# Two transformer blocks in split fp32: the high and low halves of stationary weights stored side by side

## The chip, the cores and the metric

The kernel runs on one core of a Trainium2 chip. The metric is the device time of one execution in microseconds. The kernel before took 1435.29 us (median of three runs, 1434.83 to 1439.27).

## The reference

Two models follow each other on 256 rows of 1024 features. All is fp32. The first block is a mixer (pooling and windowed attention) and an MLP:

```python
h2 = _rmsnorm(x, g_mlp_pre[l])
ff = jnp.einsum('bsf,fd->bsd',
                jnp.square(jax.nn.relu(jnp.einsum('bsd,df->bsf', h2, w_up[l]))), w_down[l])
x = x + _rmsnorm(ff, g_mlp_post[l])
```

The second has two layers, on 256 latent rows and 256 context rows. Layer 0 is a short convolution and a gated feed-forward on both sets of rows; layer 1 is attention with compressed keys and a feed-forward on the latent rows alone:

```python
def swiglu(h, w_gate, w_up, w_down):
    return (jax.nn.silu(h @ w_gate) * (h @ w_up)) @ w_down

def short_conv_mixer(h, w_in, conv_k, conv_b, w_out):
    b_gate, c_gate, u = jnp.split(h @ w_in, 3, axis=-1)
    z = c_gate * u
    ...
    return (b_gate * y) @ w_out
```

## The kernel before, in words

**Split products.** The operands of every weight product are split into two parts of type fp32r: `hi` is the value rounded to that type, `lo` is what the rounding left. `product` then runs three matmuls a term: hi by hi (line 454), one of the lo parts by the other's hi (line 455), and the other way round (line 456). All three accumulate in one PSUM bank.

**Weight chunks.** Weights come in chunks of up to 128 x 4096 fp32 (2 MiB), in the order of `STREAM`. SyncE loads chunk after chunk into the two slots of `raw`. ScalarE copies a chunk into `w_hi` (line 980, two halves), VectorE subtracts and writes `w_lo` (line 1432, two halves). `w_hi` and `w_lo` have two slots each. ScalarE may write a slot once TensorE is through with the chunk before last (`gemm_done`). SyncE may refill a slot of `raw` once VectorE is through with it (`lo_ready`). TensorE waits for the first half of `lo` in `chunk` and for the second in the middle of its first product. Chunks of modulation weights are read by TensorE from `raw` and are not split.

**Stationary and moving.** A matmul first loads a stationary operand (128 columns, the PEld rows of the profile), then streams a moving one. In the trace's names the moving operand stands first: `bank<-act_hi,w_hi` has the weights stationary. They are stationary where the result is wanted with features on partitions:

- `up` (8 chunks of the MLP), 96 matmuls a chunk, moving operand 256 columns
- `conv_in` (8 chunks of 72 matmuls a pass: the first chunk in two passes of 256 columns, the other seven in one of 512)
- `gate_up` (the feed-forward of layer 0: one chunk in two passes of 256 columns, ten chunks of 96 matmuls with 512 columns)
- `gate_up1` (the feed-forward of layer 1: 11 chunks, 96 matmuls each, 256 columns)

In all other products (projections, `down`, `down0`, `down1`, `conv_out`, attention) the activations are stationary and the weights stream.

**Order.** Each engine's program is written by hand, and semaphores join them. ScalarE and VectorE have, between the splits, the activation functions, the splits of activations, the norms and the sums. A split stands in VectorE's queue where the code puts it, so at the ends of stages it can stand ahead of the sums that the next norm needs.

Of the kernel before, what the change touches and what calls it, by code (L numbers as in the profile page):

```python
# [16 lines left out]
P = 128  # L17
D = 1024
KT = D // P
SEQ = 256  # L20
NT = SEQ // P
CHUNK = 4096
COLS = 512
# [68 lines left out]
STREAM = _stream()  # L92
WEIGHT_AT = [i for i, c in enumerate(STREAM) if not c[3]]
MOD_AT = [i for i, c in enumerate(STREAM) if c[3]]
WEIGHTS = len(WEIGHT_AT)
X_UPDATES = 16
UNITS_BEFORE_CONV = 2 * 3 + 2 + 2 * 4 + 8 + 2 + 8 + 4 + 4 * 8

# [57 lines left out]
def build(nc, a, out):  # L156
    f32, f32r = mybir.dt.float32, mybir.dt.float32r
    ACT, ALU, AX = mybir.ActivationFunctionType, mybir.AluOpType, mybir.AxisListType
# [4 lines left out]
    def at(name, shape, offset, dtype=f32):  # L163
        return nc.alloc_sbuf_tensor_at(name, shape, dtype, offset=base + offset)

    K = 1024
    raw = at("raw", [P, 2, CHUNK], 0)
    w_hi = at("w_hi", [P, 2, CHUNK], 32 * K, f32r)
    w_lo = at("w_lo", [P, 2, CHUNK], 64 * K, f32r)
    x = at("x", [P, NT, D], 96 * K)  # L170
    ACT0 = 104 * K
    act_hi = at("act_hi", [P, 2, KT, SEQ], ACT0, f32r)
    act_lo = at("act_lo", [P, 2, KT, SEQ], ACT0 + 16 * K, f32r)
# [44 lines left out]
    mlp = at("mlp", [P, NT, D], PH + 24 * K)  # L218
# [49 lines left out]
    def table(name, n, parts=P, j=0):  # L268
        return tab[0:parts, TAB[name] + j:TAB[name] + j + n]
# [18 lines left out]
    hi_ready = S("hi_ready")  # L288
# [52 lines left out]

    WQ, WKV = QKT * GH * QK, KVT * COLS

    def halves_of(width):


        half = width // 2
        return [(h * half, (h + 1) * half) for h in range(2)]

    with nc.Block() as block:  # L350
# [3 lines left out]
        def _(sp):  # L354
# [37 lines left out]
            for t in range(NT):  # L392
                sp.wait_ge(x_ready, X_UPDATES - NT + 1 + t)
                sp.dma_start(out[t * P:(t + 1) * P, :], x[:, t, :]).then_inc(out_done, 16)
# [21 lines left out]
        def _(te):  # L416
            n = Count()

            def chunk():
                n.step("chunk")  # L420
                split_half(1)
                return (n.n["chunk"] - 1) % 2
# [3 lines left out]
                te.wait_ge(lo_ready, 2 * n.at("chunk") - back)  # L426

            def weights(s, j0, j1):
                return w_hi[:, s, j0:j1], w_lo[:, s, j0:j1]

            rot = {"first": 0, "banks": 4}

# [5 lines left out]
            def unit():  # L438
                n.step("unit")
                if n.n["unit"] > rot["banks"]:  # L440
                    te.wait_ge(gemm_read, n.at("unit", rot["banks"]))
                return bank[(n.n["unit"] - 1 - rot["first"]) % rot["banks"]]
# [31 lines left out]
            def turn_rows(buf):  # L474
                te.wait_ge(xn_ready, n.step("xn"))
                for half in range(2):
                    turn([xn[:, buf, (4 * half + j) * P:(4 * half + j + 1) * P] for j in range(4)])
# [39 lines left out]
            for k, width in enumerate((COLS, COLS, 256)):  # L517
                s = chunk()
# [113 lines left out]
            def up(first=False):  # L632

                s = chunk()
                if first:
                    te.wait_ge(norm_ready, n.step("norm", 4))
                for pair in range(2):
                    b = unit()
                    for f in (2 * pair, 2 * pair + 1):
                        last = product(b[:, (f % 2) * SEQ:(f % 2 + 1) * SEQ],  # L640
                                       [(weights(s, j * COLS + f * P, j * COLS + (f + 1) * P), (act_hi[:, 0, j, :], act_lo[:, 0, j, :]))
                                        for j in range(KT)], second=4 if f == 0 else None)
                    last.then_inc(gemm_done, 1)
                n.step("hidden", 2)
# [31 lines left out]
            def moving(k):  # L676
                return act_hi[:, :, k, :], act_lo[:, :, k, :]

            def conv_weights(s, part):
                return [weights(s, k * 384 + part * P, k * 384 + (part + 1) * P) for k in range(KT)]  # L680

            def conv_in():
                s = chunk()
# [9 lines left out]
            s = chunk()  # L693
# [48 lines left out]
            s = chunk()  # L742
            for tt in range(2 * NT):
                conv_out(s, tt, tt == 0)
            s = chunk()
            norm_both(lambda tt: conv_out(s, tt, False), True)

            def gate_up(apart=False):

                s = chunk()  # L750
                for f in range(2):
                    for part in range(2):
                        b = unit()
                        cols_of = [weights(s, k * COLS + part * 256 + f * P, k * COLS + part * 256 + (f + 1) * P) for k in range(KT)]
                        half = 4 if f == part == 0 else None
                        if apart:
                            product(b[:, 0:SEQ], [(cols_of[k], (act_hi[:, 0, k, :], act_lo[:, 0, k, :])) for k in range(KT)], second=half)
                            if f == 0:
                                turn_rows(part)
                        else:  # L760
                            product(b[:, :].rearrange("p (s t) -> p s t", s=2), [(cols_of[k], moving(k)) for k in range(KT)],
                                    second=half).then_inc(gemm_done, 1)
                if apart:
                    mod_product(1, 2)
                    te.wait_ge(norm_ready, n.step("norm", 4))
                    for f in range(2):
                        for part in range(2):
                            cols_of = [weights(s, k * COLS + part * 256 + f * P, k * COLS + part * 256 + (f + 1) * P) for k in range(KT)]
                            product(bank[2 * f + part][:, SEQ:2 * SEQ], [(cols_of[k], (act_hi[:, 1, k, :], act_lo[:, 1, k, :])) for k in range(KT)]
                                    ).then_inc(gemm_done, 1)  # L770
                            gate_rows(4, f, part)
# [33 lines left out]
            s = chunk()  # L805
# [7 lines left out]
            for c in range(3):  # L813
                s = chunk()
                for tt in range(2 * NT if c == 2 else NT):
# [3 lines left out]
                    first = 0 if tt < NT else MLA_W - KVL - ROPE  # L819
# [19 lines left out]
            held = {}  # L839
# [78 lines left out]
            def gate_up1():  # L918

                s = chunk()  # L920
                for f in range(2):
                    b = unit()
                    for part in range(2):
                        first = part * 256 + f * P
                        last = product(b[:, part * SEQ:(part + 1) * SEQ],
                                       [(weights(s, j * COLS + first, j * COLS + first + P), (act_hi[:, 0, j, :], act_lo[:, 0, j, :]))
                                        for j in range(KT)], second=4 if f == part == 0 else None)
                    last.then_inc(gemm_done, 1)
                n.step("hidden", 2)
# [25 lines left out]
            down1(1, 2, 0)  # L955
            assert n.n["chunk"] == WEIGHTS and n.n["mod"] == len(MOD_AT) and n.n["batch"] == 8


        @block.scalar
        def _(act):  # L960
            n = Count()

            def split(width=CHUNK, rest=None):
                n.step("split")
                c = n.n["split"]
                if c > WEIGHTS:
                    return
                assert STREAM[WEIGHT_AT[c - 1]][2] == width, (c, width)
                s, at = (c - 1) % 2, WEIGHT_AT[c - 1]
                turns = 16 * (at // 2 + 1)  # L970
                if n.turn is not None:
                    turns = n.turn * (8 * n.per["split"]) + turns
                act.wait_ge(loaded[at % 2], turns)
                if rest is not None:
                    act.wait_ge(rest_loaded[rest], 16)
                if n.n["unit"]:
                    act.wait_ge(gemm_done, n.at("unit"))
                for first, end in halves_of(width):
                    part = slice(first, end)
                    act.activation(w_hi[:, s, part], raw[:, at % 2, part], ACT.Copy).then_inc(hi_ready, 1)  # L980

            def roots(sources, width):

# [432 lines left out]
        def _(ve):  # L1416
# [7 lines left out]
            def split(width=CHUNK):  # L1424
                n.step("split")
                if n.n["split"] > WEIGHTS:
                    return
                s, at = (n.n["split"] - 1) % 2, WEIGHT_AT[n.n["split"] - 1]
                for half, (first, end) in enumerate(halves_of(width)):
                    part = slice(first, end)  # L1430
                    ve.wait_ge(hi_ready, 2 * n.at("split") - 1 + half)
                    ve.tensor_tensor(w_lo[:, s, part], raw[:, at % 2, part], w_hi[:, s, part].bitcast(f32),  # L1432
                                     ALU.subtract).then_inc(lo_ready, 1)

            rot = {"first": 0, "banks": 4}
# [124 lines left out]
            for t in range(NT):  # L1560
# [3 lines left out]
                s = table("sin1", 8, j=8 * t).rearrange("p (o d) -> p o d", o=1).to_broadcast([P, 10, 8])  # L1564
# [634 lines left out]
```

## Time and profile before

| | |
|---|---|
| median of three runs | 1435.29 us |
| profiled execution, its own time | 1439.03 us |
| its span, first to last instruction | 1437.2 us |
| mean granted TensorE clock | 0.975 |
| TensorE busy, share of the span | 93% |
| TensorE's weight load busy | 78% |
| VectorE, ScalarE busy | 56%, 38% |
| mean of the DMA | 152 GB/s |

The profiled execution is 1.8 us longer than its span, and 3.7 us over the median of the runs. The duration of one matmul in the trace includes its latency, so neighbours overlap; the pace of a stream is read from the starts of the first and the last matmul. The granted clock is 1.00 at 2.4 GHz and 0.50 at 1.2 GHz.

### The profile page before, as it was taken

To read this page: it belongs to the slowest core of one execution; us is meant where nothing else is said; L and a number is where in the kernel's file an instruction comes from. 1 tells how busy PE (TensorE), PEld (TensorE's weight loads), DVE (VectorE), ACT (ScalarE), POOL (GpSimd) and SP (SyncE) were. 2 spreads that over 40 slices of the span, in tenths; PEclk is the share of its full clock that TensorE was granted. 3 is DMA by queue.
4 is the path that set the end of the run, shared out by engine and by line. 5 is a ranking of instruction groups with operands and counts; after the bars stand their busy time and mean duration, and the time that the engine had idled before them with its cause. 6 is when DMAs were issued, how large, how long until landed. Compare 5 with 4: busy or idle time off the path is not lost.

```text
span 1437.2 us, 17619 instructions
## 1 busy us (share of the span) xinstructions
PE 1342.5 (93%) x7376; PEld 1116.1 (78%) x7376; DVE 803.8 (56%) x1087; ACT 544.6 (38%) x679; POOL 3.5 (0%) x10
## 2 busy tenths in 40 slices
PE   5999779999999999999999999998789988799998
PEld 4877678899777788877777777887667766699997
DVE  5666565458664455662525252537556664656666
ACT  5353343454431123422121212125455552544432
POOL 0000000000000000000000000000000000000000
PEclk9999979999999999999999999999889998899999
DMA  8536436545644532363535353412121311345441
GB/s 307 192 117 251 174 110 249 213 176 180 230 154 197 205 117 88 135 245 127 226 124 227 124 227 125 150 43 92 33 87 48 117 59 59 117 159 194 175 175 59
DMA packets 23782, 218.80 MB, mean 152 GB/s; under 512 B 3104, under 2 KB 8224, under 8 KB 10656
## 3 DMA queue, kind: packets, MB, share of 16 engines
q1 hardware_dynamic: 21328, 209.67, 40.2%
q10 hardware_dynamic: 1520, 4.98, 0.9%
q0 software_dynamic: 864, 3.15, 0.7%
q8 instruction: 53, 0.87, 0.2%
q14 instruction: 17, 0.14, 0.0%
HBM read 216.74 MB, written 1.05 MB: 152 GB/s over the span
## 4 chain that ended last, share of the span: by engine, by line
PE 77%; DVE 12%; ACT 7%; issue 3%; DMA 1%; ACTq 0%; DVEq 0%
PE bank L454 23%; PE bank L455 22%; PE bank L456 22%; DVE w_lo L1432 4%; PE turned L471 3%; PE mod_ps L492 3%; ACT w_hi L980 2%; DVE scaled L1473 2%; PE bank L861 2%; PE small L867 2%; DVE gated L1778 1%; DMA raw<-in_w_branch 1%; ACT xn L987 1%; PE small L511 1%; DMA raw<-in_w_out 1%
## 5 line engine op out<-in xcount | busy, mean ns | idle before, releaser
L454 PE MATMUL bank<-act_hi,w_hi 128*128 128x256 f32 (+1 forms) x1208 | 399.7, 331 | 8.8 <-DVE act_lo L1457 6.3
L455 PE MATMUL bank<-act_lo,w_hi 128*128 128x256 f32 (+1 forms) x1208 | 395.8, 328 | 0.0
L456 PE MATMUL bank<-act_hi,w_lo 128*128 128x256 f32 (+1 forms) x1208 | 395.5, 327 | 0.0
L1432 DVE TENSOR_TENSOR w_lo<-raw,w_hi 128x2048 fp32r<-128x2048 f32 (+4 forms) x168 | 338.2, 2055 | 89.8 <-ACT w_hi L980 89.7
L980 ACT ACTIVATE w_hi<-raw 128x2048 fp32r<-128x2048 f32 (+4 forms) x168 | 280.1, 1715 | 210.0 <-PE bank L456 169.7
L454 PEld LDWEIGHTS bank<-act_hi,w_hi 128*128 128x128 f32 x1208 | 231.8, 192 | 42.8 <-issue 17.0
L455 PEld LDWEIGHTS bank<-act_lo,w_hi 128*128 128x128 f32 x1208 | 232.0, 192 | 19.5 <-issue 0.7
L456 PEld LDWEIGHTS bank<-act_hi,w_lo 128*128 128x128 f32 x1208 | 231.8, 192 | 19.3
L454 PE MATMUL bank<-w_hi,h_hi 128*128 128x512 f32 x392 | 155.4, 396 | 4.0 <-DVE h_lo L1830 2.3
L455 PE MATMUL bank<-w_lo,h_hi 128*128 128x512 f32 x392 | 153.4, 391 | 0.0
L456 PE MATMUL bank<-w_hi,h_lo 128*128 128x512 f32 x392 | 153.3, 391 | 0.0
L454 PE MATMUL bank<-w_hi,act_hi 128*128 128x512 f32 (+3 forms) x240 | 92.2, 384 | 9.6 <-DVE w_lo L1432 5.6
L454 PEld LDWEIGHTS bank<-w_hi,h_hi 128*128 128x128 f32 x392 | 74.0, 189 | 26.5 <-issue 7.7
L1827 DVE TENSOR_TENSOR h<-silu,bank 128x512 f32<-128x512 f32 x22 | 15.1, 688 | 141.5 <-PE bank L456 141.5
L455 PE MATMUL bank<-w_lo,act_hi 128*128 128x512 f32 (+3 forms) x240 | 89.5, 373 | 0.0
L456 PE MATMUL bank<-w_hi,act_lo 128*128 128x512 f32 (+3 forms) x240 | 89.4, 372 | 0.0
L1778 DVE TENSOR_TENSOR gated<-bank,gate 128x512 f32<-128x512 f32 x84 | 57.8, 688 | 53.6 <-PE bank L456 53.4
L456 PEld LDWEIGHTS bank<-w_hi,h_lo 128*128 128x128 f32 x392 | 74.0, 189 | 15.8
L455 PEld LDWEIGHTS bank<-w_lo,h_hi 128*128 128x128 f32 x392 | 74.1, 189 | 14.9 <-issue 0.2
L454 PEld LDWEIGHTS bank<-w_hi,act_hi 128*128 128x128 f32 x240 | 46.8, 195 | 19.3 <-DVE w_lo L1432 6.3
L1254 ACT ACTIVATE h_hi<-h 128x512 fp32r<-128x512 f32 x22 | 13.9, 631 | 122.2 <-DVE h L1827 122.2
L471 PE MATMUL turned<-tab,xn 128*128 128x128 f32 x156 | 24.9, 311 | 30.5 <-ACT xn L996 27.2
(227 smaller groups left out, 1421.5 us busy)
## 6 DMA issues: line engine op xcount, KB each, us to landing
raw<-in_ffn SPq DMA_DIRECT2D x35, 2048.0 KB, 8.1
raw<-in_mlp SPq DMA_DIRECT2D x24, 2048.0 KB, 8.0
raw<-in_mod_gate SPq DMA_DIRECT2D x7, 2048.0 KB, 8.1
raw<-in_conv_in SPq DMA_DIRECT2D x8, 1536.0 KB, 7.1
raw<-in_w_gates SPq DMA_DIRECT2D x4, 2048.0 KB, 8.5
raw<-in_w_branch SPq DMA_DIRECT2D x4, 2048.0 KB, 7.9
raw<-in_mla_q SPq DMA_DIRECT2D x4, 1152.0 KB, 5.3
raw<-in_w_in SPq DMA_DIRECT2D x2, 2048.0 KB, 14.0
```

The lines of the kernel that those rows point to most:

```text
L454: te.matmul(dst, sh, mh, start=(j == 0), stop=False)
L455: te.matmul(dst, sh, ml, start=False, stop=False)
L456: last = te.matmul(dst, sl, mh, start=False, stop=(j == len(terms) - 1))
L471: last = te.transpose(dst[0:m, j * P:(j + 1) * P], src, ident)
L492: last = te.matmul(mod_ps[q:q + 32, :], cond[:, k, 6 - 2 * j:38 - 2 * j], raw[:, slot, k * COLS:(k + 1) * COLS], start=(j == 0 and k < 4), ...
L861: te.matmul(bank[u % 2][:, :], qgT[:, h, t * P:(t + 1) * P], kgT[:, h, :], start=True, stop=True).then_inc(scores_done, 1)
L867: last = te.matmul(small[:, u * VD:(u + 1) * VD], prT[:, u % 2, j, :], vg[:, j, h, :], start=(j == 0), stop=(j == 3))
L980: act.activation(w_hi[:, s, part], raw[:, at % 2, part], ACT.Copy).then_inc(hi_ready, 1)
L1432: ve.tensor_tensor(w_lo[:, s, part], raw[:, at % 2, part], w_hi[:, s, part].bitcast(f32), ALU.subtract).then_inc(lo_ready, 1)
L1473: last = ve.tensor_scalar(dst[:, j, :], src[:, j, :], gain[:, j, :], shift[:, j, :], ALU.mult, ALU.add)
L1778: ve.tensor_tensor(gated[:, k, :], b[:, :], gate[:, g, cb * COLS:(cb + 1) * COLS], ALU.mult).then_inc(gemm_read, 1)
L1827: ve.tensor_tensor(h2[:, f, :], silu[:, f, :], b[:, :], ALU.mult).then_inc(gemm_read, 2)
```

## The change

The two tensors `w_hi` and `w_lo` become one region of 64 KiB a partition, with 32 KiB a slot. It has two views. `w_apart` holds the hi part of a chunk and then its lo part, each contiguous. `w_pair` holds hi and lo of an element next to each other, so that one part is read and written with a step of two elements (8 bytes). A function `held` tells by section and number which view a chunk has: the MLP's up chunks, `conv_in`, and the gate and up chunks of both feed-forwards are in pairs, all others apart. In the list above these are 38 chunks; 76 of the 168 split instructions on ScalarE and as many on VectorE write (and VectorE reads) with the step, and 3624 weight loads of TensorE read with it. The number, the order, the shapes and the waits of the instructions are the same on all engines.

```diff
+FFN1_DOWN = (4, 7, 10, 13, 15)
+def held(section, k):
+
+    if section == "mlp":
+        return k % 6 < 4
+    if section == "ffn0":
+        return k % 4 in (0, 2) and k != 18 or k == 17
+    if section == "ffn1":
+        return k not in FFN1_DOWN
+    return section in ("conv_in", "ffn0_first")
...
-    w_hi = at("w_hi", [P, 2, CHUNK], 32 * K, f32r)
-    w_lo = at("w_lo", [P, 2, CHUNK], 64 * K, f32r)
+    w_apart = at("w_apart", [P, 2, 2, CHUNK], 32 * K, f32r)
+    w_pair = at("w_pair", [P, 2, CHUNK, 2], 32 * K, f32r)
...
+    def high_half(at, s, part):
+        section, k = STREAM[at][0:2]
+        return w_pair[:, s, part, 0] if held(section, k) else w_apart[:, s, 0, part]
+
+    def low_half(at, s, part):
+        section, k = STREAM[at][0:2]
+        return w_pair[:, s, part, 1] if held(section, k) else w_apart[:, s, 1, part]
...
             def weights(s, j0, j1):
-                return w_hi[:, s, j0:j1], w_lo[:, s, j0:j1]
+                return w_apart[:, s, 0, j0:j1], w_apart[:, s, 1, j0:j1]
+
+            def held_weights(s, j0, j1):
+
+                return w_pair[:, s, j0:j1, 0], w_pair[:, s, j0:j1, 1]
...
-                                       [(weights(s, j * COLS + f * P, j * COLS + (f + 1) * P), (act_hi[:, 0, j, :], act_lo[:, 0, j, :]))
+                                       [(held_weights(s, j * COLS + f * P, j * COLS + (f + 1) * P), (act_hi[:, 0, j, :], act_lo[:, 0, j, :]))
...
-                    act.activation(w_hi[:, s, part], raw[:, at % 2, part], ACT.Copy).then_inc(hi_ready, 1)
+                    act.activation(high_half(at, s, part), raw[:, at % 2, part], ACT.Copy).then_inc(hi_ready, 1)
...
-                    ve.tensor_tensor(w_lo[:, s, part], raw[:, at % 2, part], w_hi[:, s, part].bitcast(f32),
+                    ve.tensor_tensor(low_half(at, s, part), raw[:, at % 2, part], high_half(at, s, part).bitcast(f32),
```

The same replacement of `weights` by `held_weights` stands in `conv_weights`, `gate_up` (two places) and `gate_up1`.

## Rows read from the trace of the kernel before

**Rows 1.** The page: busy time, and the chain that ended last.

```profile
PE 1342.5 (93%) x7376; PEld 1116.1 (78%) x7376; DVE 803.8 (56%) x1087; ACT 544.6 (38%) x679; POOL 3.5 (0%) x10
...
PE 77%; DVE 12%; ACT 7%; issue 3%; DMA 1%; ACTq 0%; DVEq 0%
```

**Rows 2.** Waits of TensorE: us in total, times, longest.

```profile
PE bank L454 <- DVE w_lo L1432: 7.5, 3, 3.7
```

**Rows 3.** Groups by shape: count, busy us, mean ns; of each triple the first.

```profile
L1432 DVE TENSOR_TENSOR w_lo<-raw,w_hi 128x2048 fp32r<-128x2048 f32 x124 | 278.5, 2288 | 75.8 <-ACT w_hi L980 75.8
...
L980 ACT ACTIVATE w_hi<-raw 128x2048 fp32r<-128x2048 f32 x124 | 230.0, 1903 | 200.1 <-PE bank L456 159.9 <-DMA raw<-in_mlp 14.1 <-DMA raw<-in_ffn 10.9
L454 PE MATMUL bank<-act_hi,w_hi 128*128 128x256 f32 x720 | 208.2, 289 | 8.8 <-DVE act_lo L1457 6.3 <-issue 2.5
...
L454 PE MATMUL bank<-act_hi,w_hi 128*128 128x512 f32 x488 | 191.5, 392 | 0.0
```

**Rows 4.** TensorE in order of time: start, us; held weights, 256 columns, full clock.

```profile
1257.78 0.28 PE L454 MATMUL bank<-act_hi,w_hi 128*128 128x256 f32 x1
...
1271.70 0.28 PE L456 MATMUL bank<-act_hi,w_lo 128*128 128x256 f32 x1
```

**Rows 5.** The same, held weights, 512 columns, full clock.

```profile
657.02 0.39 PE L455 MATMUL bank<-act_lo,w_hi 128*128 128x512 f32 x1
...
678.35 0.39 PE L456 MATMUL bank<-act_hi,w_lo 128*128 128x512 f32 x1
```

**Rows 6.** The same, held weights, 256 columns, half clock.

```profile
191.92 0.41 PE L456 MATMUL bank<-act_hi,w_lo 128*128 128x256 f32 x1
...
196.82 0.36 PE L455 MATMUL bank<-act_lo,w_hi 128*128 128x256 f32 x1
```

**Rows 7.** Stretches: length, busy PE, PEld, DVE, ACT, POOL, granted clock, DMA.

```profile
640.00:900.00 260.00, 260.00 (x1226) 200.17 (x1225) 102.58 (x106) 60.55 (x56) 0.00 (x0) 1.00 0.48 173
191.70:196.80 5.10, 5.10 (x25) 5.10 (x25) 5.07 (x3) 2.42 (x2) 0.00 (x0) 0.50 0.00 0
1258.00:1284.00 26.00, 26.00 (x219) 26.00 (x218) 13.25 (x15) 12.90 (x16) 0.00 (x0) 1.00 0.44 163
...
1243.90:1248.40 4.50, 4.50 (x21) 4.50 (x22) 3.46 (x2) 4.09 (x3) 0.00 (x0) 0.51 0.02 4
```

**Rows 8.** In order of time: eight transposes; seven weight loads with 64 moving columns each.

```profile
577.38 1.03 PE L471 MATMUL turned<-tab,xn 128*128 128x128 f32 x8
...
1112.46 0.86 PEld L867 LDWEIGHTS small<-vg,prT 128*128 128x128 f32 x7 [0.24 <-issue]
```

**Rows 9.** Groups: VectorE reductions of 128 elements, first with, second without a step.

```profile
L1513 DVE TENSOR_REDUCE fold<-turned 128x32 f32<-128x128 f32 x4 | 1.1, 284 | 0.0
...
L1889 DVE TENSOR_REDUCE stat<-pe_t 128x4 f32<-128x128 f32 x1 | 0.3, 286 | 0.0
```

**Rows 10.** ScalarE and VectorE in order of time, feed-forward of layer 1.

```profile
1258.89 3.70 ACT L980 ACTIVATE w_hi<-raw 128x2048 fp32r<-128x2048 f32 x2
...
1260.82 4.49 DVE L1432 TENSOR_TENSOR w_lo<-raw,w_hi 128x2048 fp32r<-128x2048 f32 x2 [1.38 <-ACT w_hi L980]
...
1270.41 3.71 ACT L980 ACTIVATE w_hi<-raw 128x2048 fp32r<-128x2048 f32 x2
```

**Rows 11.** The chain in order of time: start, us, what.

```profile
165.08 1.93 ACT w_hi L980
167.10 3.38 DVE w_lo L1432 x2
...
559.96 1.93 ACT w_hi L980
561.92 3.48 DVE w_lo L1432 x2
...
1222.27 1.93 ACT w_hi L980
1224.22 4.49 DVE w_lo L1432 x2
```

**Rows 12.** DMA issues: count, KB each, us to landing.

```profile
raw<-in_ffn SPq DMA_DIRECT2D x35, 2048.0 KB, 8.1
```

More of the change, by code:

```diff
@@ L679, in conv_weights @@
             def conv_weights(s, part):
-                return [weights(s, k * 384 + part * P, k * 384 + (part + 1) * P) for k in range(KT)]
+                return [held_weights(s, k * 384 + part * P, k * 384 + (part + 1) * P) for k in range(KT)]
             def conv_in():
@@ L753, in gate_up @@
                         b = unit()
-                        cols_of = [weights(s, k * COLS + part * 256 + f * P, k * COLS + part * 256 + (f + 1) * P) for k in range(KT)]
+                        cols_of = [held_weights(s, k * COLS + part * 256 + f * P, k * COLS + part * 256 + (f + 1) * P) for k in range(KT)]
                         half = 4 if f == part == 0 else None
@@ L767, in gate_up @@
                         for part in range(2):
-                            cols_of = [weights(s, k * COLS + part * 256 + f * P, k * COLS + part * 256 + (f + 1) * P) for k in range(KT)]
+                            cols_of = [held_weights(s, k * COLS + part * 256 + f * P, k * COLS + part * 256 + (f + 1) * P) for k in range(KT)]
                             product(bank[2 * f + part][:, SEQ:2 * SEQ], [(cols_of[k], (act_hi[:, 1, k, :], act_lo[:, 1, k, :])) for k in range(KT)]
@@ L925, in gate_up1 @@
                         last = product(b[:, part * SEQ:(part + 1) * SEQ],
-                                       [(weights(s, j * COLS + first, j * COLS + first + P), (act_hi[:, 0, j, :], act_lo[:, 0, j, :]))
+                                       [(held_weights(s, j * COLS + first, j * COLS + first + P), (act_hi[:, 0, j, :], act_lo[:, 0, j, :]))
                                         for j in range(KT)], second=4 if f == part == 0 else None)
```

## The prediction

> **What bounds the kernel now.** I read the page's busy times and its chain first: TensorE is busy for 93% of the span and carries 77% of the chain, VectorE 12% and ScalarE 7% [rows 1]. TensorE's waits come next: all its waits for the lo part of a weight chunk are 7.5 us, in three places [rows 2]. So in the long stages the end is set by how fast TensorE runs its matmuls, and the splits run beside it. The stretches say the same: in 640 to 900 us and in 1258 to 1284 us TensorE is busy for the whole stretch at a granted clock of 1.00, and VectorE for 39% and 51% of it [rows 7].
>
> What the change touches on TensorE is counted in the groups by shape: 720 triples with 256 moving columns and 488 triples with 512 have the weights stationary, so 2160 and 1464 matmuls, each with its own load [rows 3]. Their pace is read from starts. With 256 columns, 116 intervals lie between 1257.78 and 1271.70: 13.92 us / 116 = 120.0 ns [rows 4]. With 512, 94 intervals (the rest of a chunk of 96 matmuls) take 21.33 us: 226.9 ns [rows 5]. The columns alone need 256/2.4 = 106.7 ns and 512/2.4 = 213.3 ns. So each matmul has a surcharge of 13.3 and 13.6 ns that does not grow with its columns. At the granted clock of 0.50 (1.2 GHz) it is gone: 23 intervals in 4.90 us are 213.0 ns, and 256/1.2 is 213.3 ns [rows 6, 7]. Something that is no part of the array's own work, and that has room at half clock, costs 13.3 ns at full clock. In all it is 3624 x 13.3 ns = 48.2 us, 3.3% of the run. That is the largest thing the change can give on TensorE.
>
> **Part 1, the stationary load reads with a step of 8 bytes.** The trace has no such load, so this is bounded from both sides.
> How fast a load goes at best is seen where almost nothing streams: seven loads with 64 moving columns take 0.86 us. Less the 0.19 us of the last one, that is 0.67/6 = 112 ns for 128 columns. Eight transposes take (1.03 - 0.28)/7 = 107 ns each [rows 8]. So a load reads some 512 bytes in 107 to 112 ns, 4.6 to 4.8 bytes per ns and partition, and the moving stream reads 1024 bytes in 106.7 ns, 9.6 bytes per ns. The two run at the same time, through the same memory, and the load walks its addresses at half the pace of the stream. A surcharge that depends on neither width nor, at half clock, exists at all fits two readers that run into each other again and again while one overtakes the other. With a step of 8 bytes the load walks 1024 bytes in the same time, at the stream's own pace: once they are out of each other's way they stay so. That is an inference and not a row. It gives a gain of up to the whole surcharge. Against that stands the other reading of the same rows, a fixed gap between two moving streams, which a step in the load doesn't touch: gain zero. And the load now covers twice the memory: if the surcharge is paid per stretch of memory touched, it doubles.
> Gain if the first holds: with 512 columns I take 12 of the 13.6 ns, 1464 x 12 = 17.6 us. With 256 columns the load's own pace comes next: from 120.0 to 109 ns (the middle of 107 and 112), 2160 x 11 = 23.8 us. Some 46 matmuls run at half clock and gain nothing (25 and 21 in two stretches [rows 7]): -0.5 us. Sum 40.9 us.
>
> The Trainium skill ("SBUF — State Buffer", section "Who interferes with whom") says that TensorE has two independent read ports, one for the moving operand and one for the load, and never waits on anyone. By that rule the surcharge is no meeting of the two reads, and the whole change is worth nothing: the time would stay that of before. The trace neither shows nor excludes it, so it bears on the chance of "no change" below.
>
> **Part 2, ScalarE and VectorE write with the step, and VectorE reads with it.** 76 of the 168 splits on each. A half of 2048 elements now takes 2288 ns on VectorE and 1903 ns on ScalarE [rows 3]. The nearest row for a step is a reduction of 128 elements 32 words apart (in PSUM): 284 ns, against 286 ns without a step [rows 9]. So I take zero. The lower end is also zero: nothing is removed. As the upper end I take double time, since each half now lies over twice the memory.
> What hides it is seen in the feed-forward of layer 1: a split starts on ScalarE at 1258.89 and the next at 1270.41, 11.5 us apart, one chunk of 96 x 120 ns. The hi halves end 3.7 us after the start, the lo halves 6.4 us after it (1260.82 + 4.49 = 1265.31) [rows 10]. TensorE wants the chunk some 10.3 us after that start and its second half 1.4 us later (12 matmuls at 120 ns): 5 us of slack, 4 us if TensorE's chunk shrinks to 10.5 us. The DMA has 8.1 us to land [rows 12] within two chunks. Nothing else becomes late.
> If the cover goes, it goes first at the three stage ends where a held chunk's split stands in the chain: 1.93 + 3.38, 1.93 + 3.48 and 1.93 + 4.49 us, together 17.1 us [rows 11]. At double time these cost 17 us more. Between stages the second lo half would come 1.9 x 2 + 4.5 x 2 = 12.8 us after the start, against 11.7 wanted: 1.1 us on each of 19 chunks with 256 columns (mlp and layer 1), 21 us. So the upper end of part 2 is +38 us.
>
> The Trainium skill has two rules on it that differ. "SBUF — State Buffer", section "Specifications (TRN2)", wants at least two accesses to a 16-byte line for full bandwidth; a step of 8 bytes has exactly two, so it would be free, and the reduction's row doesn't contradict. "Vector Engine (DVE) Microarchitecture Reference", section 5.2, measured 1.7 times the duration where the destination hops with every 4-byte element; at that factor the three stage ends would cost 12 us, which is my rival on that side in kind.
>
> **Part 3, the other chunks.** Their halves are contiguous as before; only the distance from hi to lo is 16 KiB instead of 32. Zero, both ends.
>
> **The sum.** 1439.0 (profiled) - 40.9 + 0 = 1398.1 us. The median of the runs is 3.7 us below the profiled execution, so 1394.4 us. At stage ends and in the last MLP turn the chain goes through the splits and sums, and there TensorE's gain is partly waited away; I give 3 us back for it: 1398 us is the forecast.
>
> **The rivals.**
> No change. The surcharge is a gap between moving streams or a cost of changing the weights, whatever their layout. For it: it is the same for widths of 256 and 512. Against: it vanishes at half clock, where a cost of the array would double. Time 1435.3 us, give or take 3.
> Slower, by the load's reach. The surcharge is paid per stretch of memory that a load touches, and the stretch doubles from 512 to 1024 bytes: +13.3 ns on all 3624 matmuls, +48 us, 1484 us. It decides from the first held chunk on, in every one. For it: a fixed surcharge on a fixed load. Against: nothing in particular.
> Slower, by the splits. Part 2 between 1.7 times and double: +12 to +38 us, 1447 to 1473 us. Against it stands the reduction's row.
> Slower, by the load's pace. If a stepped load needs double time, 107 ns become 213, hidden under 512 columns (226.9 ns) but not under 256: there 120 becomes 227, 2160 x 107 ns = +231 us, 1666 us. The unstepped load already goes at half the stream's byte rate, so I hold it for unlikely.
>
> **How the numbers follow.** My forecast (a gain on TensorE) 0.50; no change 0.28; load's reach 0.10; splits 0.08; load's pace 0.04. A measurement of this kernel tells about 0.3% from no change (4.3 us). So faster 0.50, same 0.28, slower 0.22. The forecast's own range is 1385 (the whole 48 us and nothing given back) to 1420 (a third of it). The range that holds 8 in 10 also takes in no change and the small end of the splits: 1385 to 1446.
>
> **What would show each step right or wrong.** Starts of held matmuls at 109 ns and 215 ns in place of 120 and 227, with the moving-weight products still at 226 to 227, show part 1; unchanged paces show the fixed gap; 133 and 240 show the reach; 227 with 256 columns shows the load's pace. The groups of the splits at 2288 and 1903 ns with the step show part 2 right; 3.9 us and more shows it wrong. The forecast fails if the paces move and the span doesn't: then the splits or the DMA must stand in TensorE's waits.

## The result, and the profile after

The changed kernel is slower: 1450.32 us (median of 5 runs, 1448.77 to 1453.27) against 1439.27 us for the kernel before on the same chip (5 runs, 1434.83 to 1441.97). The ratio is 1.0084, 95% interval 1.0067 to 1.0101. The forecast was 1398 us, and 1450.3 lies above its range as well. The profiled span went from 1437.2 to 1447.0 us, +9.8 us, at nearly the same mean granted clock (0.975 before, 0.972 after).

The page of the changed kernel, busy time and chain, which answer to [rows 1]:

```profile
PE 1352.9 (94%) x7376; PEld 1125.2 (78%) x7376; DVE 803.6 (56%) x1087; ACT 558.5 (39%) x679; POOL 3.5 (0%) x10
...
PE 76%; DVE 12%; ACT 7%; issue 3%; DMA 2%; ACTq 0%; DVEq 0%
```

TensorE is busy 10.4 us longer and ScalarE 13.9 us; VectorE is unchanged. TensorE's waits for lo parts have not moved, 7.5 us as in [rows 2] (waits: us in total, times, longest):

```profile
PE bank L480 <- DVE w_apart L1458: 7.5, 3, 3.7
```

So it is the matmuls, not the splits. The groups by shape of the changed kernel, which answer to [rows 3]:

```profile
L480 PE MATMUL bank<-act_hi,w_pair 128*128 128x256 f32 x720 | 208.8, 290 | 8.4 <-DVE act_lo L1483 5.9 <-issue 2.5
...
L480 PE MATMUL bank<-act_hi,w_pair 128*128 128x512 f32 x488 | 193.8, 397 | 0.0
...
L1458 DVE TENSOR_TENSOR w_apart<-raw,w_apart 128x2048 fp32r<-128x2048 f32 x64 | 143.7, 2287 | 39.5 <-ACT w_apart L1006 39.5
L1458 DVE TENSOR_TENSOR w_pair<-raw,w_pair 128x2048 fp32r<-128x2048 f32 x60 | 134.8, 2290 | 41.6 <-ACT w_pair L1006 41.6
L1006 ACT ACTIVATE w_pair<-raw 128x2048 fp32r<-128x2048 f32 x60 | 122.9, 2104 | 165.3 <-PE bank L482 140.5 <-DMA raw<-in_mlp 14.3 <-DMA raw<-in_ffn 10.5
L1006 ACT ACTIVATE w_apart<-raw 128x2048 fp32r<-128x2048 f32 x64 | 118.6, 1902 | 30.5 <-PE bank L482 14.5 <-PE bank L559 6.5 <-DMA raw<-in_w_branch 6.0
```

The products with 256 columns are as they were (290 against 289 ns), those with 512 last 397 against 392 ns. VectorE's stepped halves take 2290 against 2287 ns: free. ScalarE's take 2104 against 1902 ns: +10.6%, 202 ns each.

A matmul's own duration overlaps its neighbours', so the pace is again read from starts. The changed kernel with 256 columns, to be held against [rows 4] (start, us, ...):

```profile
1265.09 0.28 PE L481 MATMUL bank<-act_lo,w_pair 128*128 128x256 f32 x1
...
1279.97 0.28 PE L482 MATMUL bank<-act_hi,w_pair 128*128 128x256 f32 x1
```

124 intervals in 14.88 us are 120.0 ns, exactly as before. With 512 columns, against [rows 5]:

```profile
663.17 0.39 PE L482 MATMUL bank<-act_hi,w_pair 128*128 128x512 f32 x1
...
684.17 0.40 PE L482 MATMUL bank<-act_hi,w_pair 128*128 128x512 f32 x1
```

90 intervals in 21.00 us are 233.3 ns; before they were 226.9. That is +6.4 ns, and 1464 x 6.4 ns = 9.4 us, nearly the whole +9.8 us of the span. The stage can be cut out of both traces. The first held product with 512 columns and the first matmul behind the last one, before:

```profile
410.14 0.50 PE L454 MATMUL bank<-act_hi,w_hi 128*128 128x512 f32 x1
...
961.66 0.39 PE L454 MATMUL bank<-w_hi,h_hi 128*128 128x512 f32 x1
```

and after:

```profile
411.49 0.50 PE L480 MATMUL bank<-act_hi,w_pair 128*128 128x512 f32 x1
...
972.17 0.39 PE L480 MATMUL bank<-w_apart,h_hi 128*128 128x512 f32 x1
```

Between them lie 551.5 us before and 560.7 after: +9.2 us. What comes ahead took 1.4 us longer, what comes behind 0.7 us less. The 1.4 us ahead are the clock's: behind its waits at the start of the convolution, TensorE ran 17 matmuls with 256 columns at a granted clock of 0.50 in this execution, 0.21 us apart in place of 0.12. The same products of the kernel before ran at 1.00. The stretch (length, busy PE, PEld, DVE, ACT, POOL, granted clock, DMA):

```profile
400.90:404.20 3.30, 3.30 (x17) 3.30 (x17) 3.10 (x5) 0.68 (x1) 0.00 (x0) 0.50 0.00 0
```

At the three stage ends, the chain of the changed kernel, which answers to [rows 11]:

```profile
164.76 2.07 ACT w_pair L1006
...
166.92 3.25 DVE w_pair L1458 x2
...
564.41 2.08 ACT w_pair L1006
...
1232.13 2.09 ACT w_pair L1006
...
1234.24 4.50 DVE w_pair L1458 x2
```

ScalarE's part grew by 0.14 to 0.16 us at each, under 0.5 us in all.

### The profile page after: what moved, and what is told of

The parts are those of the page before. It is cut to its first block, busy times and chain, and to the rows that moved or that the text cites. A ratio compares the mean times of both kernels' runs of the same rounds, so it can differ in the third digit from the quotient of the medians.

```text
span 1447.0 us, 17619 instructions
## 1 busy us (share of the span) xinstructions
PE 1352.9 (94%) x7376; PEld 1125.2 (78%) x7376; DVE 803.6 (56%) x1087; ACT 558.5 (39%) x679; POOL 3.5 (0%) x10
## 3 DMA queue, kind: packets, MB, share of 16 engines
HBM read 216.74 MB, written 1.05 MB: 151 GB/s over the span
## 4 chain that ended last, share of the span: by engine, by line
PE 76%; DVE 12%; ACT 7%; issue 3%; DMA 2%; ACTq 0%; DVEq 0%
PE bank L480 23%; PE bank L481 22%; PE bank L482 22%; DVE w_apart L1458 3%; PE turned L497 3%; PE mod_ps L518 3%; ACT w_apart L1006 2%; DVE scaled L1499 2%; DVE w_pair L1458 2%; PE bank L887 2%; PE small L893 2%; ACT w_pair L1006 1%; DVE gated L1804 1%; DMA raw<-in_w_branch 1%; ACT xn L1013 1%
## 5 line engine op out<-in xcount | busy, mean ns | idle before, releaser
L480 PE MATMUL bank<-act_hi,w_pair 128*128 128x256 f32 (+1 forms) x1208 | 402.6, 333 | 8.4 <-DVE act_lo L1483 5.9
L481 PE MATMUL bank<-act_lo,w_pair 128*128 128x256 f32 (+1 forms) x1208 | 398.4, 330 | 0.0
L482 PE MATMUL bank<-act_hi,w_pair 128*128 128x256 f32 (+1 forms) x1208 | 398.3, 330 | 0.0
L480 PEld LDWEIGHTS bank<-act_hi,w_pair 128*128 128x128 f32 x1208 | 237.5, 197 | 42.9 <-issue 17.0
L481 PEld LDWEIGHTS bank<-act_lo,w_pair 128*128 128x128 f32 x1208 | 237.7, 197 | 19.9 <-issue 0.7
L482 PEld LDWEIGHTS bank<-act_hi,w_pair 128*128 128x128 f32 x1208 | 237.4, 196 | 19.5
L1006 ACT ACTIVATE w_pair<-raw 128x2048 fp32r<-128x2048 f32 (+1 forms) x76 | 148.2, 2005 | 171.1 <-PE bank L482 146.3
L1458 DVE TENSOR_TENSOR w_apart<-raw,w_apart 128x2048 fp32r<-128x2048 f32 (+4 forms) x92 | 175.9, 1954 | 47.8 <-ACT w_apart L1006 47.7
L1458 DVE TENSOR_TENSOR w_pair<-raw,w_pair 128x2048 fp32r<-128x2048 f32 (+1 forms) x76 | 162.3, 2178 | 48.5 <-ACT w_pair L1006 48.5
L480 PE MATMUL bank<-w_apart,h_hi 128*128 128x512 f32 x392 | 154.8, 395 | 5.7 <-DVE h_lo L1856 2.3
L481 PE MATMUL bank<-w_apart,h_hi 128*128 128x512 f32 x392 | 152.7, 390 | 0.0
L482 PE MATMUL bank<-w_apart,h_lo 128*128 128x512 f32 x392 | 152.7, 390 | 0.0
L480 PE MATMUL bank<-w_apart,act_hi 128*128 128x512 f32 (+3 forms) x240 | 92.4, 385 | 9.6 <-DVE w_apart L1458 5.6
L481 PE MATMUL bank<-w_apart,act_hi 128*128 128x512 f32 (+3 forms) x240 | 89.6, 373 | 0.0
L1280 ACT ACTIVATE h_hi<-h 128x512 fp32r<-128x512 f32 x22 | 13.9, 633 | 125.4 <-DVE h L1853 125.4
```

The costliest lines, as they stand in the source:

```text
L480: te.matmul(dst, sh, mh, start=(j == 0), stop=False)
L481: te.matmul(dst, sh, ml, start=False, stop=False)
L482: last = te.matmul(dst, sl, mh, start=False, stop=(j == len(terms) - 1))
L1006: act.activation(high_half(at, s, part), raw[:, at % 2, part], ACT.Copy).then_inc(hi_ready, 1)
L1458: ve.tensor_tensor(low_half(at, s, part), raw[:, at % 2, part], high_half(at, s, part).bitcast(f32), ALU.subtract).then_inc(lo_ready, 1)
```

## Experiments

The prediction's theory was that a stepped load runs in step with the stream and removes the surcharge of 13.3 ns. The profile after had already refuted it, since no pace went down. The question became why 512 columns rose by 6.4 ns and 256 did not, and whether the surcharge has to do with addresses at all. The rival was that it is a fixed gap that no layout moves, with the loss coming from somewhere else (the new places of the halves, or ScalarE).

**The pace by itself.** A program of matmul bursts: the same stationary block and the same moving columns, 36 times, with the step, the width or the distance of the two start addresses changed from burst to burst.

```
for n, steps in ((256, (1, 2, 4)), (384, (1, 2)), (512, (1, 2, 4, 8))):
    for step in steps:
        configs.append([(stat(W, step), mov(M, n), n)] * R)
```

> A program of its own that leaves out the whole model: it streams bursts of 36 to 48 matmuls on operands at rest, no other engine at work, and then runs ScalarE copies and VectorE subtractions with and without a step. Theory A (the step of the stationary load alone costs, when the moving operand is 512 wide): a step of 2 gives 233 ns against 227 at 512 columns in one piece, and 120 against 120 at 256. Theory B (it is the moving operand in two pieces together with the step): 227 and 227 in one piece, 227 and 233 in two pieces. Theory C (addresses of the two operands relative to each other): the pace changes with the offset of the stationary operand at step 1 too, between 120 and 133, 227 and 240. Theory D (the surcharge needs the other engines or the DMA): 227 in all cases, whatever the step. ScalarE: 1.90 us without a step, 2.10 with a step of 2; VectorE 2.29 us in both.

Its TensorE in order of time; each burst (bank) stands between two small marks, and its pace is the start of the next mark less its own start, over 36:

```profile
42.38 4.56 PE L267 MATMUL bank<-mem 128*128 128x256 f32 x36
46.77 0.31 PE L264 MATMUL mark<-mem 128*128 128x64 f32 x2
46.91 4.57 PE L267 MATMUL bank<-mem 128*128 128x256 f32 x36
51.32 0.31 PE L264 MATMUL mark<-mem 128*128 128x64 f32 x2
51.46 8.65 PE L267 MATMUL bank<-mem 128*128 128x256 f32 x36
59.95 0.30 PE L264 MATMUL mark<-mem 128*128 128x64 f32 x2
...
73.02 8.43 PE L267 MATMUL bank<-mem 128*128 128x512 f32 x36
81.29 0.30 PE L264 MATMUL mark<-mem 128*128 128x64 f32 x2
81.43 8.65 PE L267 MATMUL bank<-mem 128*128 128x512 f32 x36
89.92 0.30 PE L264 MATMUL mark<-mem 128*128 128x64 f32 x2
90.05 8.82 PE L267 MATMUL bank<-mem 128*128 128x512 f32 x36
98.71 0.30 PE L264 MATMUL mark<-mem 128*128 128x64 f32 x2
```

With 256 columns: 121.9 ns without a step, 122.5 with a step of 2 elements, 235.8 with 4. With 512: 229.7, 235.8 and 240.6. (Such a burst reads some 2 ns too long, since its first matmul starts slowly: the kernel's 120.0 is 121.9 here. The granted clock is 1.00 throughout.) So both of the kernel's numbers are here with no split, no DMA and no other engine at work: a step of 2 costs 0.6 ns at 256 and 6.1 ns at 512. With the 512 columns in two pieces of 256, as in the kernel, it is 229.4 without and 235.6 with the step, so the two pieces are not the cause. Without a step, moving the stationary block by 4, 8, 16 or 32 elements gave 235.8, 235.8, 235.3 and 234.7 ns at 512 as well; by 64, 128, 256, 1024 or 4096 elements 229.2 to 229.4. So the pace with 512 columns depends on where the load starts, modulo 64 elements (256 bytes). That it is the distance to the stream, and not the load's own alignment, is shown by the bursts under "Which distances". With a step, no distance gave less than 232.8.

A half of 2048 elements copied by ScalarE took 1.91 us without a step, 2.04 us (+6.6%) with a step of 2, and 3.81 us with a step of 4; VectorE took 2.29 us in every form, steps of 1 and 2 in its input and its output.

**The new places, without pairs.** The layout of the changed kernel, but every chunk apart, and TensorE's loads with it. (This edit and the next two are shown against the changed kernel.)

```
-    if section == "mlp":
-        return k % 6 < 4
...
-    return section in ("conv_in", "ffn0_first")
+    return False
```

> The memory layout of the change (hi and lo of a slot 16 KiB apart) with no chunk in pairs. If the step is the cause: as before, 1439 us within 0.3%, held matmuls with 512 columns at 227 ns. If the nearness of hi and lo is the cause: as the change, 1450 us and 233 ns.

1439.29 us, ratio 0.9998 (0.9986 to 1.0011). In order of time:

```profile
657.45 0.40 PE L476 MATMUL bank<-act_hi,w_apart 128*128 128x512 f32 x1
...
678.55 0.39 PE L476 MATMUL bank<-act_hi,w_apart 128*128 128x512 f32 x1
```

93 intervals in 21.10 us are 226.9 ns. Part 3 of the prediction stands: the distance of 16 KiB costs nothing that these runs show.

**Pairs only where 256 columns stream** (the MLP and layer 1).

```
-    return section in ("conv_in", "ffn0_first")
+    return section == "mlp" and k % 6 < 4 or section == "ffn1" and k not in FFN1_DOWN
```

> Pairs only where the held matmuls have 256 columns throughout (MLP up, feed-forward of layer 1). If the cost is the 6.4 ns on each of the 1464 matmuls with 512 columns: as before, 1439 to 1441 us. If ScalarE's slower stepped write (2.10 against 1.90 us a half) at the ends of stages is the cause: 0.4 us at each of two stage ends, 1440 us, and the rest of the 11 us unexplained. If the whole change costs evenly per held matmul: 1439 + 11 x 1824/3624 = 1444.5 us.

1439.59 us, ratio 1.0006 (0.9995 to 1.0016); pace 120.0 ns. ScalarE paid its +10.6% here too, on 38 of the 76 stepped halves, and nothing came of it: the split's cover held.

**Pairs only where 512 columns stream** (the convolution's input and the feed-forward of layer 0).

```
-    if section == "mlp":
-        return k % 6 < 4
...
-    if section == "ffn1":
-        return k not in FFN1_DOWN
```

> Pairs only in conv_in and in the gate and up chunks of layer 0, where 1464 of 1800 held matmuls have 512 columns. If those 1464 x 6.4 ns = 9.4 us are the cause: 1448 to 1450 us, nearly the whole loss. If the cost is even per held matmul: 1444.5 us.

1447.81 us, ratio 1.0054 (1.0041 to 1.0067). By shape, that program's held products (all its 488 triples with 512 columns are from pairs, the 608 with 256 from chunks apart):

```profile
L476 PE MATMUL bank<-act_hi,w_pair 128*128 128x512 f32 x488 | 193.8, 397 | 0.0
...
L476 PE MATMUL bank<-act_hi,w_apart 128*128 128x256 f32 x608 | 174.3, 287 | 6.7 <-DVE act_lo L1479 4.2 <-issue 2.5
```

The 397 ns of the changed kernel, and most of its loss. The two halves of the change add up to 1.0060, the whole measured 1.0084; their intervals leave it open whether a rest of about 0.2% is real. The half-clock stretch at 400.9 us, worth 1.5 us in the profile of the whole change, is in neither half's profile; whether such stretches make up the rest is not shown.

**Which distances.** Bursts as above, at twelve distances with and without a step, at six more widths, and with both blocks moved together.

```
for n, step in ((256, 1), (512, 1), (256, 2), (512, 2)):
    for off in (0, 4, 8, 12, 16, 20, 24, 28, 32, 40, 48, 56):
        configs.append([(stat(W + off, step), mov(M, n), n)] * R)
```

> Again a program of its own that leaves out the whole model: bursts of matmuls on operands at rest, swept over the start address of the stationary operand (in elements of 4 bytes), its step, the width, and the start of the moving operand. The theory that two readers of one memory meet expects a pace that depends on the difference of the two start addresses within 256 bytes, and so the same pace for both moved by 64 bytes as for neither (120 and 227 ns, with some 2 ns for the start of a burst on top). A theory in which only the load's own alignment counts expects (16, 16) to go as (16, 0). A fixed gap between streams expects 120 and 227 everywhere at step 1, which the first sweep has already put in doubt (offset 64 bytes: 116 at 256 columns, 235 at 512). If the cost of the step belongs to wide streams, it begins at one width between 384 and 512.

Its TensorE in order of time, without a step: 256 columns at distances of 12 and 16 elements, then 512 at 0 and 16:

```profile
55.27 4.49 PE L264 MATMUL bank<-mem 128*128 128x256 f32 x36
59.60 0.31 PE L261 MATMUL mark<-mem 128*128 128x64 f32 x2
59.74 4.34 PE L264 MATMUL bank<-mem 128*128 128x256 f32 x36
63.92 0.30 PE L261 MATMUL mark<-mem 128*128 128x64 f32 x2
...
95.53 8.41 PE L264 MATMUL bank<-mem 128*128 128x512 f32 x36
103.78 0.30 PE L261 MATMUL mark<-mem 128*128 128x64 f32 x2
...
129.78 8.64 PE L264 MATMUL bank<-mem 128*128 128x512 f32 x36
138.27 0.30 PE L261 MATMUL mark<-mem 128*128 128x64 f32 x2
```

256 columns: 120.3 ns at 12, 116.1 at 16. 512 columns: 229.2 at 0, 235.8 at 16. Then 512 columns with both blocks moved by 16 elements:

```profile
493.14 8.45 PE L264 MATMUL bank<-mem 128*128 128x512 f32 x36
501.43 0.30 PE L261 MATMUL mark<-mem 128*128 128x64 f32 x2
```

That is 230.3 ns (122.2 with 256 columns), near the 229.2 of distance 0 and not the 235.8 of the moved load alone, so it is the distance that counts. The two reads do meet. Of the twelve distances, 0 is the best for 512 columns, and it is the one at which the kernel's tiles already lie; for 256 columns 16 is better than 0. One burst does not fit at 256: with the stream moved by 48 elements, which is again distance 16 modulo 64, the pace was 120.3 and not 116.1 ns (at 512 it was 235.6, as it should be). With a step of 2 all twelve distances lie between 120.6 and 123.6 ns at 256 and between 232.5 and 236.1 at 512: with the step, no distance reaches the better level. The cost of the step belongs to the widest streams: at 480 columns there was none (219.2 ns both ways), at 496 it was 2.2 ns (225.6 and 227.8).

**Every distance.** The same without a step, all 64 distances, bursts of 24.

```
for off in range(64):
    configs.append([(stat(W + off), mov(M, 256), 256)] * 24)
```

> A program of its own without the model: bursts of 24 matmuls with 256 and then 512 moving columns, the stationary operand's start swept over all 64 elements of 256 bytes, step 1. If two readers meet, the pace depends on the distance of their starts and takes few levels, some 6.7 ns apart: at 256 columns 113 ns at the best distance and 120 at distance 0, at 512 columns 227 at 0 and 233 elsewhere. The question is whether any distance brings 512 columns under 227 ns (220 or 213).

At 512 columns most distances lie at 234 to 238 ns and none under 230.4 (these shorter bursts read 3 to 4 ns too long). Distance 0 gave 231.2, and 30, 33 and 60 gave the same within 0.8 ns (230.4, 230.5, 230.9), so 0 is one of four good ones. At 256 most lie at 120 to 124, two at 117.5 and 117.9 (19 and 42 elements), and distance 16 was 121.2 this time. So the better level at 256 is not set by the distance alone. This program leaves open where the levels lie and why; it does show that no distance removes the surcharge.

**The distance alone, in the kernel: 256 columns.** The kernel before, with the activations of the MLP and of layer 1 lying 64 bytes earlier; no pairs. (This edit and the next are shown against the kernel before. The other tensors behind them move by a multiple of 256 bytes.)

```
+    moved_hi = at("moved_hi", [P, 2, KT, SEQ], ACT0 + -64, f32r)
...
-  (weights(s, ...), (act_hi[:, 0, j, :], act_lo[:, 0, j, :]))
+  (weights(s, ...), (moved_hi[:, 0, j, :], moved_lo[:, 0, j, :]))
```

> No pairs and no step: the kernel before with the activations 64 bytes nearer to the start, in the MLP and in the feed-forward of layer 1, so that weights and moving activations (256 columns) start at another distance within 256 bytes. If the distance counts as in three of the four bursts at 64 bytes (113.5 in place of 120.0 ns): 1824 matmuls x 6.5 ns = 11.9 us faster, 1427 us. If that level was luck of the phase, as the fourth burst (120 ns) hints: no change, 1439 us.

1434.42 us against 1438.82, ratio 0.9971 (0.9958 to 0.9985): faster than both kernels. Its TensorE in order of time, in layer 1 and then in the MLP's second pair of chunks:

```profile
1250.04 0.28 PE L458 MATMUL bank<-moved_hi,w_lo 128*128 128x256 f32 x1
...
1285.97 0.28 PE L457 MATMUL bank<-moved_lo,w_hi 128*128 128x256 f32 x1
...
240.09 0.28 PE L456 MATMUL bank<-moved_hi,w_hi 128*128 128x256 f32 x1
...
255.99 0.28 PE L456 MATMUL bank<-moved_hi,w_hi 128*128 128x256 f32 x1
```

317 intervals in 35.93 us are 113.3 ns; 135 in 15.90 us are 117.8. Each chunk keeps one of these two paces to its end. Both were in the bursts at distance 16 as well: read from the third matmul on, three of the plain bursts ran at 113.4 to 113.6 ns, and two at 117.8 (the one that did not fit, and that of the last program). Of the 1824 products 960 are in chunks of the first kind and 864 in chunks of the second, so the gain on them is some 960 x 6.7 + 864 x 2.2 ns = 8.3 us, and the span fell by 6.7. The median fell by 4.4 us only, against the 11.9 us expected. A stretch without any such product gave something back in the profiled execution: the attention of layer 1, first in the kernel before, then here (length, busy PE, granted clock, DMA):

```profile
1120.00:1160.00 40.00, 35.45 (x208) 1.00 0.29 106
```

```profile
1116.00:1156.00 40.00, 37.36 (x207) 0.91 0.29 105
```

Nearly two microseconds more busy for the same work, at a lower granted clock in this one execution. From the end of layer 0's held products to the first of layer 1 it took 284.6 us against 282.2.

**The distance alone, in the kernel: 512 columns.** The same for the convolution's input and layer 0, 192 bytes later, which is the same distance modulo 256 bytes. (Here the tensors behind the activations move by 448 bytes, which is not a multiple of 256.)

```
+    moved_hi = at("moved_hi", [P, 2, KT, SEQ], ACT0 + 192, f32r)
```

> No pairs and no step: the kernel before with the activations of conv_in and of layer 0's feed-forward moved by 192 bytes. If the loss of the change is a meeting of two readers that depends on how their addresses run past each other, a distance alone must cost the same: 233 ns in place of 227 on 1464 matmuls with 512 columns, +9.4 us, less up to 2.2 us on the 336 with 256 columns: 1446 to 1449 us. If only the step costs: 1439 us and 227 ns.

1447.49 us, ratio 1.0052 (1.0034 to 1.0070). Its TensorE in order of time:

```profile
661.13 0.39 PE L456 MATMUL bank<-moved_hi,w_hi 128*128 128x512 f32 x1
...
682.59 0.39 PE L458 MATMUL bank<-moved_hi,w_lo 128*128 128x512 f32 x1
```

92 intervals in 21.46 us are 233.3 ns. Without any step or pair, a loss of the same size is there: 233.3 ns, and 1.0052 against 1.0054 for the pairs.

**Step and distance together.** Pairs in the MLP and layer 1, and their activations 64 bytes earlier (the edit against the changed kernel).

```
-  (held_weights(s, ...), (act_hi[:, 0, j, :], act_lo[:, 0, j, :]))
+  (held_weights(s, ...), (moved_hi[:, 0, j, :], moved_lo[:, 0, j, :]))
```

> The stationary chunks of the MLP and of layer 1 lie side by side (as in the program where only these did), and their activations lie 64 bytes earlier against the weights (as in the program with the changed distance alone, where the pace of these 256-column products fell from 120.0 to 113.3 ns and the time by 0.3%). Theory A (a stepped load runs past its whole 256-byte stretch against the stream, so it takes away whatever a distance gives): the pace is 120.0 ns again in 1241 to 1287 us, and the time is that of before within 0.2% (ratio 1.000). Theory B (the distance of the start addresses decides, whatever the step): 113.3 ns and the time 0.3% under that of before (0.997).

1440.55 us, ratio 1.0007 (0.9995 to 1.0019). In order of time:

```profile
1260.11 0.28 PE L477 MATMUL bank<-moved_lo,w_pair 128*128 128x256 f32 x1
...
1289.99 0.28 PE L477 MATMUL bank<-moved_lo,w_pair 128*128 128x256 f32 x1
```

249 intervals in 29.88 us are 120.0 ns. The step takes away what the distance gives, as in the bursts.

## Why the prediction was wrong, point by point

**What bounds the kernel** was right: TensorE's pace in the held products sets the end, and its change by 6.4 ns is seen in the time nearly one for one.

**Part 1 failed, at its inference.** The words were: "With a step of 8 bytes the load walks 1024 bytes in the same time, at the stream's own pace: once they are out of each other's way they stay so." The premise, that the load and the stream run into each other, is borne out: the pace depends on the distance of their start addresses while nothing else runs (229.2 against 235.8 ns). The step from there to lockstep is what fell. With the step the surcharge stayed 13.3 ns at 256 columns, and at 512 it rose from 13.6 to 20.0 ns. -40.9 us was forecast and +9.4 us came. What the argument did not ask was whether the present layout already had a good distance at 512. It had: distance 0 modulo 256 bytes, where none of the 64 was better by more than 0.8 ns. A load that steps over 1024 bytes has no fixed distance to the stream in units of 256 bytes and misses the better level whatever its start. That last sentence is my reading; shown are the paces (every distance tried with a step at 232.5 to 236.1 ns, 0 and multiples of 64 elements without one at 229).

The Trainium skill ("SBUF — State Buffer", section "Who interferes with whom") gives TensorE two independent read ports and lets it never wait on anyone. By that rule the change is worth nothing. The trace agrees at 256 columns (120.0 ns before and after) and not at 512, and the bursts disagree: 229.2 against 235.8 ns for nothing but another start address of the load. The measurement decides.

**Part 2.** VectorE at zero was right (2290 against 2287 ns). ScalarE at zero was wrong: +10.6%, 202 ns a half. (Alone it was +6.6%, 2.04 against 1.91 us; what adds the rest in the kernel is not shown.) I had taken one engine's row, a reduction on VectorE, for both engines. The cover that the prediction described held: pairs in the MLP and layer 1 alone gave 1.0006. The three stage ends paid under 0.5 us, within the 0 to 17 us given there.

The Trainium skill ("SBUF — State Buffer", section "Specifications (TRN2)") wants two accesses to a 16-byte line. With a step of 2 elements there are two, with 4 there is one: ScalarE's copy took 1.91, 2.04 and 3.81 us with steps of 1, 2 and 4, and the matmuls with 256 columns 121.9, 122.5 and 235.8 ns. That agrees with the rule but for ScalarE's extra at a step of 2 (10.6% in the kernel). The 6.1 ns of the step with 512 columns do not agree with it. VectorE, with steps of 1 and 2 only, took 2.29 us in both, which agrees too.

The prediction's 1.7 times left out its condition. The table of the Trainium skill ("Vector Engine (DVE) Microarchitecture Reference", section 5.2) has 1.71 ns a column, against 1.05 where all is contiguous, for a destination that hops 4 KiB with every element. That is 1.6 times, and another step than this one. At a step of 2 elements nothing of it showed on VectorE (2290 against 2287 ns).

**Part 3** was right: ratio 0.9998.

**The rivals.** "No change" (0.28) held for the 2160 products with 256 columns, 120.0 ns before and after, but not for its reason: a fixed gap between streams would not turn into 113.3 ns when the activations move by 64 bytes. The rival of the load's reach (+13.3 ns on all 3624, 1484 us) had the sign and the engine. It was wrong in the size, half a surcharge, and in the place, only the 1464 products with 512 columns. I gave it 0.10 and wrote that nothing spoke against it. The splits' rival had the time (1447 to 1473) but not the cause: TensorE's waits for lo parts are the same 7.5 us. Its price was +12 to +38 us, and the change cost 11.0 on the same chip. A load of half the pace did not come at a step of 2; the bursts with a step of 4 show what it would have been, 235.8 ns at 256 columns against the 227 of that rival.

**The range** ended at 1446 because the two slower mechanisms on TensorE were priced only at a full surcharge or a doubled load. A part of a surcharge, in one of two widths, was the missing case: 1464 x 6.7 ns = 9.8 us, 1445 to 1449 us. The base was low as well: three runs gave 1435.3 us for the kernel before, the larger sets of the experiments 1438.8 to 1439.4, so every time in the prediction stands some 4 us too low.

Still open: why the surcharge exists at full clock and at every distance, which of two levels a chunk with 256 columns falls into at distance 16, and the rest of about 0.2% between the whole change and its two halves.

## What to carry to other kernels

Two streams that run through the same memory can depend on the distance of their addresses. Before a layout is changed to make them agree, a program of bursts with nothing but the two streams, at several distances and steps, separates what a profile of the whole kernel can't. It gives the direction more surely than the size: the bursts promised 11.9 us from 64 bytes, and the kernel gained 4.4. And a layout may already sit at a good distance, where moving or spreading a tile loses it; where it doesn't sit there (here 256 columns), 64 bytes are worth trying first.

## What the runs showed of the hardware

- The pace of back-to-back fp32r matmuls with their loads settled at a few levels in the kernels at full clock: 113.3 and 120.0 ns at 256 columns, 226.9 and 233.3 at 512, which is 6.6, 13.3, 13.6 and 20.0 ns over the columns' own 106.7 and 213.3: steps of some 6.7 ns, 16 periods of 2.4 GHz. Between them stands 117.8 ns, kept through whole chunks. In bursts other distances lay between these levels, such as 231.7 ns at 48 elements with 512 columns.
- In bursts without any other engine, 512 columns ran at 229.2 or 235.8 ns by the distance of the load's start from the stream's, modulo 256 bytes.
- A step of 4 elements in the load doubled the time per matmul with 256 columns (121.9 to 235.8 ns) and added 10.9 ns with 512 (229.7 to 240.6); a step of 8 with 512 gave 250.0.
- At widths of 320 to 480 a step of 2 made no difference over 1.4 ns in either direction (416 columns: 190.8 without, 189.4 with; 480 columns: 219.2 and 219.2).
- ScalarE writes fp32r with a step of 2 elements 10.6% slower in the kernel (2104 against 1902 ns for 2048) and 6.6% slower alone (2.04 against 1.91 us), VectorE at the same pace.
